# Looking up expert numbers among fewer candidates, and another share of the expert adds for VectorE

## The reference, cut to what matters

```python
v1, i1 = lax.top_k(s1, PEER_TOPK)          # per head, 16 of 128 keys
v2, i2 = lax.top_k(s2, PEER_TOPK)
cand_s = v1[..., :, None] + v2[..., None, :]           # 16 x 16 sums
cand_i = i1[..., :, None] * N_KEYS + i2[..., None, :]
best_s, pos = lax.top_k(cand_s, PEER_TOPK)
expert = jnp.take_along_axis(cand_i, pos, axis=-1)
gate = jax.nn.softmax(best_s, axis=-1)
u, vv = down[expert], up[expert]           # rows of 1024 floats each
act = gelu(u . t);  out = sum(gate * act * vv)
```

## Time and profile before

| | us |
|---|---|
| median of 3 runs | 4257.76 |
| lowest, highest | 4244.02, 4261.35 |
| the profiled execution | 4251.79 |
| its span | 4250.0 |
| TensorE busy | 3255.1 (77%) |
| VectorE busy | 2905.9 (68%) |
| ScalarE busy | 1418.3 (33%) |
| mean granted TensorE clock | 0.864 of full |

### The profile page before, as it was taken

One profiled execution on the slowest core, in us unless ns is written; L12 is line 12 of the kernel. 1 busy time (PEld: TensorE's weight loads), 2 busy tenths in 40 slices (PEclk: granted clock), 3 DMA queues, 4 the chain that ended last, 5 costly groups with the idle time before them and its releaser, 6 DMA issues.

```text
span 4250.0 us, 44182 instructions
## 1 busy us (share of the span) xinstructions
PE 3255.1 (77%) x14236; PEld 1821.3 (43%) x14236; DVE 2905.9 (68%) x5934; ACT 1418.3 (33%) x4074; POOL 1435.1 (34%) x1158
## 2 busy tenths in 40 slices
PE   9996836887787787869786877788778868786656
PEld 5554533452545253526352544354344525452222
DVE  1003355759776977697679767876887597769765
ACT  1001102433352435233523352344244323523323
POOL 0000002424343344334333433343344243424554
PEclk9997667998889888979887989798989988898879
DMA  4102227999899899989997999799989997999998
GB/s 190 52 38 82 86 74 289 398 401 375 316 401 409 322 367 413 409 319 375 413 390 312 389 406 391 313 391 412 385 334 399 397 379 315 399 381 362 422 422 370
DMA packets 223286, 1413.08 MB, mean 332 GB/s; under 512 B 25619, under 2 KB 34323, under 8 KB 72134
## 3 DMA queue, kind: packets, MB, share of 16 engines
q0 software_dynamic: 165888, 1208.03, 70.4%
q1 hardware_dynamic: 55878, 190.35, 11.7%
q10 hardware_dynamic: 1296, 11.94, 0.7%
HBM read 1391.06 MB, written 20.41 MB: 332 GB/s over the span
## 4 chain that ended last, share of the span: by engine, by line
DVE 32%; PE 26%; DMA 14%; ACT 6%; issue 5%; POOL 1%; another core or an unknown queue 0%; DVEq 0%; SPq 0%; POOLq 0%; PEldq 0%; ACTq 0%
DVE ex_rows L1495 14%; PE mx_ps L1469 10%; DMA ex_rows<-experts,ex_expert_c 9%; PE mx_ps L1213 4%; DVE ex_x2c L1505 2%; DMA mx_fac<-w_q 2%; DMA mx_ex<-w_out 2%; DVE mx_pqb L1313 2%; DVE mx_fac L1314 2%; PE mx_ps L996 1%; DVE mx_pqb L1311 1%; PE mx_ps L1003 1%; PE mx_ps L960 1%; ACT ex_diag L1451 1%; PE mx_ps L1196 1%
## 5 line engine op out<-in xcount | busy, mean ns | idle before, releaser
L1432 POOL DMA_INDIRECT ex_rows<-experts,ex_expert_c x1152 | 1433.8, 1245 | 2781.9 <-PE mx_ps L1469 1283.6
L1469 PE MATMUL mx_ps<-ex_rows,ex_diag 128*128 128x512 f32 x3096 | 1650.8, 679 | 365.0 <-ACT ex_diag L1451 353.2
L1495 DVE CUSTOM_DVE_ANT_0 ex_rows<-ex_rows,ex_tnc 128x1024 f32<-128x1024 f32 x1152 | 1375.5, 1222 | 222.4 <-DMA ex_rows<-experts,ex_expert_c 206.5
L1469 PEld LDWEIGHTS mx_ps<-ex_rows,ex_diag 128*128 128x128 f32 x3096 | 628.2, 215 | 1227.8 <-issue 1223.3
L1441 ACT ACTIVATE ex_coef<-ex_coef 128x1 f32<-128x1 f32 x1152 | 222.9, 202 | 1549.4 <-DVE ex_coef L1495 1533.8
L1505 DVE SCALAR_TENSOR_TENSOR ex_x2c<-ex_rows,ex_coef,ex_x2c 128x1024 f32<-128x1024 f32 x378 | 485.3, 1284 | 136.5 <-ACT ex_coef L1444 129.4
L1444 ACT ACTIVATE ex_coef<-ex_coef,ex_gate_c 128x1 f32<-128x1 f32 x1152 | 283.7, 285 | 9.7
L1451 ACT ACTIVATE ex_diag<-cn_ident,ex_coef 128x128 f32<-128x128 f32 x774 | 283.3, 392 | 9.3
L260 PE MATMUL psP<-pj_w_in_sb,pj_hT 128*128 128x432 f32 x768 | 279.6, 526 | 0.0
L229 DVE TENSOR_SCALAR pj_proj_sb<-psP,pj_rstd_a 128x432 f32<-128x432 f32 x27 | 18.0, 668 | 277.7 <-PE psP L260 243.7
L260 PEld LDWEIGHTS psP<-pj_w_in_sb,pj_hT 128*128 128x128 f32 x768 | 145.4, 190 | 130.1 <-issue 130.1
(11 more groups left out here) (293 smaller groups left out, 3945.5 us busy)
## 6 DMA issues: line engine op xcount, KB each, us to landing
mx_fac<-w_q SPq DMA_DIRECT2D x54, 512.0 KB
mx_ex<-w_out SPq DMA_DIRECT2D x36, 512.0 KB
mx_ex<-w_q SPq DMA_DIRECT2D x36, 512.0 KB
ex_rows<-experts,ex_expert_c POOLq DMA_INDIRECT x1152
mx_p_cur<-w_q SPq DMA_DIRECT2D x27, 512.0 KB
mx_xs<-w_q SPq DMA_DIRECT2D x27, 512.0 KB
proj_rows<-pj_proj_sb ACTq DMA_DIRECT2D x9, 1296.0 KB, 4.7
mx_p_cur<-proj_rows SPq DMA_DIRECT2D x9, 1296.0 KB, 8.7
```

The costliest lines, as they stand in the source:

```text
L1432: pool.indirect_dma_start(rows[:, g % RING, :], None, A["experts"], bass.IndirectOffsetOnAxis(expert_c[:, s:s + 1], 0))\
L1469: last = pe.matmul(bank(6 + c), diag[:, n % DIAGS, :], up[:, r, c * 512:(c + 1) * 512], start=n == 0, stop=n == len(ON_PE) - 1)
L1495: dve.tensor_tensor_reduce(out=down[:, r, :], in0=down[:, r, :], in1=tnc[:, :], scale=1.0, scalar=0.0, op0=ALU.mult, op1=ALU.add, accum_ou ...
```

## The change

The list CAND is put in another order and cut into more pieces, so that its first 8 entries hold every sum that can be among the best 4, its first 20 every sum that can be among the best 8, and all 50 as before. The lookup is no longer by head but by rank: ranks 0 to 3 of all heads compare with 8 candidates, ranks 4 to 7 with 20, ranks 8 to 15 with 50, two heads at a time. That makes 6 groups of three linked instructions at marks 60, 61, 62, 63, 65 and 66 in place of 8 at marks 60 to 67, with 8 x 4 x 8 = 256, 8 x 4 x 20 = 640 and 2 x 8 x 50 = 800 elements per partition. Each list of candidates is built by 14 instructions in place of 7.

In STAGES the shares rise for marks up to 16 from 0.4 to 0.7, for 25 from 0.4 to 0.6, for 28 and 38 by 0.1, and fall to 0.2 for marks 6, 7 and from 68 on. Two slots leave the maps, one each joins 26 to 28 and leaves 49 to 59, and two join 43 to 48. The lists that follow: VectorE adds 49 of the 128 slots in place of 42.

```diff
-ROUTE_LINKS = 43
+ROUTE_LINKS = 37
...
-CAND = [(0, 1, 16), (1, 1, 8), (2, 1, 5), (3, 1, 4), (4, 1, 3), (5, 3, 2), (8, 8, 1)]
-NCAND = sum(n * m for _, n, m in CAND)
+CAND = [(0, 1, 0, 4), (1, 1, 0, 2), (2, 2, 0, 1),
+        (0, 1, 4, 4), (1, 1, 2, 2), (2, 2, 1, 1), (4, 4, 0, 1),
+        (0, 1, 8, 8), (1, 1, 4, 4), (2, 1, 2, 3), (3, 1, 2, 2), (4, 1, 1, 2), (5, 3, 1, 1), (8, 8, 0, 1)]
+NCAND = sum(n * m for _, n, _, m in CAND)
...
-STAGES = ((6, 2, 0.5), (7, 4, 0.5),
-          (16, 19, 0.4),
-          (25, 16, 0.4),
-          (28, 7, 0.2),
-          (38, 21, 0.3),
+STAGES = ((6, 2, 0.2), (7, 4, 0.2),
+          (16, 19, 0.7),
+          (25, 14, 0.6),
+          (28, 8, 0.3),
+          (38, 21, 0.4),
           (42, 5, 0.7),
-          (48, 9, 0.8),
-          (59, 17, 0.0),
+          (48, 11, 0.8),
+          (59, 16, 0.0),
           (67, 13, 0.0),
-          (71, 4, 0.3),
-          (MARKS + 1, 1, 0.5), (MARKS + 2, 0, 0.5), (MARKS + 3, 5, 0.5), (END, 5, 0.5))
+          (71, 4, 0.2),
+          (MARKS + 1, 1, 0.2), (MARKS + 2, 0, 0.2), (MARKS + 3, 5, 0.2), (END, 5, 0.2))
...
-        hot = part(pqb, 0, (TOPK, NCAND))
...
-                for a, n, w in CAND:
+                for a, n, b, w in CAND:
                     out = dst[:, :, at:at + n * w]
                     if n == 1:
-                        last = dve.tensor_tensor(out, src[:, :, 1, 0:w],
+                        last = dve.tensor_tensor(out, src[:, :, 1, b:b + w],
                                                  src[:, :, 0, a:a + 1].to_broadcast([P, 8, w]), ALU.add)
-                    elif w == 1:
+                    else:
                         last = dve.tensor_tensor(out, src[:, :, 0, a:a + n],
-                                                 src[:, :, 1, 0:1].to_broadcast([P, 8, n]), ALU.add)
-                    else:
-                        last = dve.tensor_tensor(out.rearrange("p h (n m) -> p h n m", m=w),
-                                                 src[:, :, 1, 0:w].unsqueeze(2).to_broadcast([P, 8, n, w]),
-                                                 src[:, :, 0, a:a + n].unsqueeze(3).to_broadcast([P, 8, n, w]),
-                                                 ALU.add)
+                                                 src[:, :, 1, b:b + 1].to_broadcast([P, 8, n]), ALU.add)
...
-            for h in range(8):
-                slots.upto(60 + h)
-                link(dve.tensor_tensor(hot, iota[:, :].unsqueeze(1).to_broadcast([P, TOPK, NCAND]),
-                                       posf[:, h, :].unsqueeze(2).to_broadcast([P, TOPK, NCAND]), ALU.is_equal))
-                link(dve.tensor_tensor(hot, hot, cidx[:, h, :].unsqueeze(1).to_broadcast([P, TOPK, NCAND]), ALU.mult))
-                link(dve.tensor_reduce(expf[:, h, :], hot, AX.X, ALU.add))
+            for mark, heads, ranks, n in ((60, (0, 8), (0, 4), 8), (61, (0, 8), (4, 8), 20), (62, (0, 2), (8, 16), NCAND),
+                                          (63, (2, 4), (8, 16), NCAND), (65, (4, 6), (8, 16), NCAND),
+                                          (66, (6, 8), (8, 16), NCAND)):
+                slots.upto(mark)
+                hs, rs = slice(*heads), slice(*ranks)
+                shape = [P, heads[1] - heads[0], ranks[1] - ranks[0], n]
+                at_rank = part(pqb, 0, tuple(shape[1:]))
+                link(dve.tensor_tensor(at_rank, iota[:, 0:n].unsqueeze(1).unsqueeze(1).to_broadcast(shape),
+                                       posf[:, hs, rs].unsqueeze(3).to_broadcast(shape), ALU.is_equal))
+                link(dve.tensor_tensor(at_rank, at_rank, cidx[:, hs, 0:n].unsqueeze(2).to_broadcast(shape), ALU.mult))
+                link(dve.tensor_reduce(expf[:, hs, rs], at_rank, AX.X, ALU.add))
```

## The result

The changed kernel takes **4223.8 us** (median of 8 runs, 4214.5 to 4234.2), the one before 4257.3 (8 runs): a ratio of 0.9927, interval 0.9909 to 0.9945. That is 33.5 us gained, 0.8%, where 4160 and some 99 us had been forecast; the direction is right, the size a third. The profiled execution took 4214.46 us, its span is 4212.7, its mean granted clock 0.857 (0.864 before).

What follows compares the result with a forecast made beforehand. Memory was taken as the bound, idle only 44 of 409 us per period; 6 + 5 + 1 - 0.5 = 11.5 us over eight periods plus 7.3 on the sample tile gave 99 us, so 4160 us, range 4110 to 4225.

Steps and rivals of the forecast that it cites:

- The lookup: VectorE in routing: 24.5 to 16.2 us per tile; 7.3 us net of the candidates, 6 taken per period.
- The candidates: List pieces on VectorE, 14 instead of 7, twice per tile: 1.0 us more per tile.
- The sample tile: Nothing lies beside routing there, so the whole 7.3 us come off.
- Solves and maps: VectorE carries more adds under TensorE's work in its idle time: 5 us per period, bounds 0 and 11.
- rival C: Solve steps: VectorE's moved adds ahead of line 816 lengthen the chain by 1.2 us each; 4318 us, chance 0.06.
- rival D: TensorE's clock in the solves falls as its load drops; at worst 4459 us, chance 0.02.
- The same part's rule: Throttled clock is the default, activity releases it; by it the solves' 5 us per tile are lost, some 4200.
- The turn: Turn of the tile: final sum still waits for TensorE's eight-slot lump; gathers restart sooner, 1 us gained per period.
- group norm, attention and projections: Marks 26 to 48: three more VectorE adds where memory is mostly full; 0.5 us lost per period.
- A: Only the lookup pays, the solves stay as long because rows are released in order; 4203 us, chance 0.14.

Runs made afterwards that it cites:

- e1: The changed kernel with the STAGES table of the kernel before, so the new lookup and candidates alone: 4189.7 us, ratio 0.9839 against the kernel before.
- e4: The changed kernel with VectorE's share in marks 8 to 16 at 0.5 instead of 0.7: 4160.4 us, ratio 0.9764 against the kernel before.
- e7: The changed kernel plus four unread matmuls per prompt tile where TensorE rests ahead of line 1014: 4196.3 us, ratio 0.9883 against the kernel before.
- e6: e5 with 16 slots at 0.4 in marks 17 to 25, 7 at 0.2 in 26 to 28, 17 in 49 to 59: 4153.9 us.
- e5: The changed kernel with the edits of e3 and e4 together: 4109.8 us, ratio 0.9675 against the kernel before.
- e3: The changed kernel with 9 instead of 11 slots in marks 43 to 48 and 18 instead of 16 in 49 to 59: 4178.0 us.
- e12: e5 with two slots exchanged, slot 74 on VectorE and slot 76 on TensorE: 4143.0 us, ratio 0.9739 against the kernel before.
- e8: The changed kernel with VectorE's share in marks 43 to 48 at 0.5 instead of 0.8, still 11 slots: 4198.4 us.
- e9: The changed kernel with VectorE adding slot 79 instead of slot 81, all counts as before: 4231.7 us, ratio 0.9940 against the kernel before.
- e11: e6 with slot 79 on VectorE and slot 81 on TensorE: 4160.1 us, ratio 0.9789 against the kernel before.
- e10: e1 with slot 79 on TensorE and slot 81 on VectorE: 4203.2 us, ratio 0.9893 against the kernel before.

## Why the prediction was wrong, and where it was right

**The lookup: right.** Eighteen instructions at 0.42, 0.82 and 0.99 us, as worked out. The candidates cost 1.0 us (marks 55 to 59: 19.8 us in e1, 18.8 before). The sample tile gave 7.7 us in e1 and 8.4 in after, for 7.3. In the periods I took 6 of 7.3 "since the memory comes within 3% of full"; e1 gave 8.0. That reserve was not needed, since idle memory after the turn fell too (18.3 to 13.6 us).

**The solves: the term was right, its consequence was not seen.** Marks 6 to 16 became 5.5 us shorter and the wait ahead of line 816 halved, from 111.1 to 57.9 us. But the step "Solves and maps", of which the prediction took 5 us (bounds 0 and 11), gave 1.7 (marks 6 to 25: 112.1 us before, 110.4 after). It set VectorE's extra adds against VectorE's idle time of the stretch, a mean, and did not ask at which step TensorE's cover runs out. At the last one, TensorE has no product and no add left, and the two adds ahead of line 819 lie open: 3.8 us in after, 0.7 in e4 and before, at the end of eight solves. That is rival C's mechanism, at one step where I had priced it at all seven; C needed idle time to be used up everywhere and so looked unlikely at 0.06. The rest then set off rival D at the same place: a clock of 0.57 in the 12 us behind it in five tiles of seven, and 1.00 in all of them once e7 fills the rest. Marks 17 to 28 rose from 56.2 to 64.9 us, but only 3.8 of these 8.7 us are in the maps. The other 4.9 are in marks 26 to 28, and not this rest's doing: they stay in e7 (19.8 us) and mostly in e4 (18.5), and they are gone in e6 (13.0), which gives the maps and the group norm their old entries, but there marks 29 to 42 are 4.6 us longer than in e5. The sizes: e7 gives the clock's part, 27 us (19 by the ratios); the open wait is (3.8 - 0.7) x 8 = 25, an estimate that charges every microsecond of it to the time; together 44 to 52 of the 63 us that e4 gained. The remainder was not tried apart.

**D was mispriced by its form.** I said that it "needs a fall no row shows", and reckoned with the mean load of the solves. The load was no guide: the clock fell behind a stretch in which TensorE was busy for 25 of 30 us, and e7 shows that the one rest at its end did it. The Trainium skill ("TensorE: Matmul & The Clock Gate", Part 1) says in its passage on oscillation that a wait for a DMA between groups of matmuls throttles the array again, so that the next group starts slow every time. The wait here is for VectorE. The trace agrees in five tiles of seven (0.99 ahead of the 3.8 us rest, 0.57 behind it), in part in one (0.86), and not in tile 5 (1.00), so "every time" does not hold here. The same part's rule, which I had quoted in the prediction, gave the right sign and was set aside because attention kept its clock at three quarters of load.

**The query stage: a cost put at nothing.** The prediction charged 0.5 us for "stretches where it has over 20 us free and the memory is full", marks 26 to 48, and that came out about right: 143.4 us for 143.6. What it had no cost for is marks 49 to 54, behind them, where the slots and adds of the query stage come due: 44.2 us for 38.4. Marks 43 to 54 together became 8.4 us longer; e3, which takes that entry back to nine slots, gains 46 us, against 64 us between forecast and result. I had counted adds, and not what the two slots more do to the order: gathers against the query weights, adds of TensorE behind all groups of the product, and buffers that are freed in order. What decides within this stage stays open in part: e12 shows that the places of TensorE's few slots count for 27 to 33 us with equal numbers on each engine, e8 that eleven slots with fewer adds on VectorE win half of e3's gain, e9 and e11 that it isn't slot 79 alone.

**The turn: right in its reason.** Rows of the changed kernel, TensorE's lump and the final sum:

```profile
1862.57 13.98 PE L1472 MATMUL mx_ps<-ex_rows,ex_diag 128*128 128x512 f32 x32
```

```profile
1876.66 1.22 DVE L1518 TENSOR_TENSOR ex_x2c<-ex_x2c,mx_ps 128x1024 f32<-128x1024 f32 x1 [5.44 <-PE mx_ps L1472]
```

Eight slots, 14 us, and line 1518 waits 5.4 us for them, as foretold; marks 68 to the next tile's first dot take 52.1 us for 51.5. Of the 1 us taken 0.3 was there in the six turns that another period follows (53.6 us for 53.9); the turn into the last tile, on which the prediction had no word, became 6.6 us longer.

**The sum.** By the prediction's own terms, per period: lookup 6, measured 8.6 (marks 55 to 67); solves and maps 5, measured 1.7; group norm, attention and projections -0.5, measured 0.2; marks 49 to 54 nothing, measured 5.8 lost; turn 1, measured 0.6 lost with the last one in the mean. That is 11.5 forecast and 4.1 measured. So two steps failed: the solves and maps were taken as covered by VectorE's mean idle time, and the two slots and their adds moved into the query stage were given no price in the stretch behind it. A (only the lookup pays) was nearest in time among the rivals, but not what happened: the table did not merely fail to pay, it cost 34 us. That the time lies inside the stated range of 4110 to 4225 is luck: the lookup's 2.6 us more than forecast hid part of the loss. The pace of an add, 1.2 us, for which the prediction points at its rows 8, stands in these two rows of the kernel before:

```profile
1853.67 1.28 DVE L1505 SCALAR_TENSOR_TENSOR ex_x2c<-ex_rows,ex_coef,ex_x2c 128x1024 f32<-128x1024 f32 x1
1854.87 1.22 DVE L1495 CUSTOM_DVE_ANT_0 ex_rows<-ex_rows,ex_tnc 128x1024 f32<-128x1024 f32 x1
```

## What to carry to other kernels

When work moves between two engines, don't weigh it against the idle time of a stage: go through the steps one by one, look at the last one before a handover, where the other engine has nothing left to cover the wait, and look at what TensorE's clock does behind it. Where buffers are freed in order, price each moved or added slot by what it queues behind (here a product that itself waits for weights), since its place in the order can count as much as the number of slots. And try the parts of such a change one at a time: the lookup was worth 69 us, the table cost 34, and two entries of the table mended make it worth 80 on top.

## What the runs showed of the hardware that was not expected

- Behind one rest of 3.8 us of TensorE per tile, between two dependent products, the granted clock went from 0.99 to 0.57 for the next 12 us in five tiles of seven, to 0.86 in one, and stayed at 1.00 in one; with four 512-column matmuls put into the rest, which do nothing for the result, it is 1.00 in all seven and the kernel 27 us faster (4196.3 for 4223.8; 19 by the ratios).
- In the query projection, where weight blocks of 512 KB are loaded between gathers of 1 MB, TensorE waited 1.7 us for each of five blocks in a row (48 us of such waits in after, 18 in before and in e5, none in e8, which has as many gathers in the stage as after but issues them two at a time).
- An exchange of two slots between two engines, with all counts kept, changed the time by 27 to 33 us in one kernel (e5 to e12), by 13 to 23 in another (e1 to e10), and by nothing that can be told in two more (e9, e11).
